# Expert passes of an fp32 MoE block: small-block groups one chunk sooner, one-hot picks on VectorE, two weight remainders on GpSimd

## The reference, cut to what matters

```python
logits = h @ w_router + b_router
top_v, top_i = lax.top_k(logits, 4); gates = softmax(top_v)
# tokens of each expert, in blocks of rows; for each block (idx, gate, e):
xb = xt[idx]
g = min(xb @ w_gate[e] + b_gate[e], 7.0)
u = clip(xb @ w_up[e] + b_up[e], -7.0, 7.0)
act = g * sigmoid(1.702 * g) * (u + 1)
y = (act @ w_down[e] + b_down[e]) * gate[:, None]
# the rows of y are added to their tokens
```

## Time and profile before

| | us |
|---|---|
| median of 3 runs | 2213.45 |
| lowest, highest | 2213.32, 2217.33 |
| the profiled execution | 2214.42 |
| its span, first to last instruction | 2212.7 |
| TensorE busy | 2137.0 (97%) |
| VectorE busy | 1538.9 (70%) |
| ScalarE busy | 1114.8 (50%) |
| GpSimd busy | 888.5 (40%) |
| mean granted TensorE clock | 0.988 |

### The profile page before, as it was taken

How to read it: one execution, slowest core, us unless ns; L and a number is a source line. 1 busy time by engine, 2 the same in 40 slices (tenths; PEclk the granted TensorE clock), 3 DMA queues, 4 the chain that set the end, 5 groups by cost and what they waited for, 6 DMA issues and landing times.

```text
span 2212.7 us, 37038 instructions
## 1 busy us (share of the span) xinstructions
PE 2137.0 (97%) x11540; PEld 1557.8 (70%) x11541; DVE 1538.9 (70%) x1940; ACT 1114.8 (50%) x1138; POOL 888.5 (40%) x486
## 2 busy tenths in 40 slices
PE   8999999999999969999999999999999999999997
PEld 6874554787888847777666767776776766677776
DVE  5544433535335588988777788878887877789996
ACT  4433233424222146675645656565665655566674
POOL 1343121000000045875633545555574455356761
PEclk9999999999999979999999999999999999999999
DMA  6421110233334289999878898899898898899994
GB/s 227 98 74 60 39 47 10 82 90 102 88 105 152 105 325 388 352 357 338 302 274 292 315 303 317 307 319 313 308 352 280 302 307 291 291 318 324 351 341 111
DMA packets 206010, 517.77 MB, mean 234 GB/s; under 512 B 19168, under 2 KB 86624, under 8 KB 205952
## 3 DMA queue, kind: packets, MB, share of 16 engines
q1 hardware_dynamic: 190016, 470.97, 59.2%
q0 software_dynamic: 15936, 46.02, 8.6%
HBM read 480.68 MB, written 32.05 MB: 232 GB/s over the span
## 4 chain that ended last, share of the span: by engine, by line
PE 69%; issue 8%; DVE 8%; POOL 8%; DMA 3%; DVEq 3%; ACT 1%; SPq 0%; POOLq 0%; ACTq 0%
PE psum L1689 7%; PE psum L1933 7%; PE psum L1924 6%; PE psum L1926 6%; PE psum L1901 5%; POOL pick L679 4%; PE psum L1709 4%; PE psum L1711 4%; PE psum L1710 4%; DVE late_lo L1385 3%; PE psum L1964 3%; PE psum L1966 3%; PE psum L1972 3%; PE psum L1912 2%; DMA out_rows<-ysb,idx_cur 2%
## 5 line engine op out<-in xcount | busy, mean ns | idle before, releaser
L679 POOL TENSOR_SCALAR pick<-iota_bf,slot_col 128x256 bf16<-128x256 bf16 x244 | 523.5, 2160 | 214.5 <-DVE slot_col L1403 214.5
L1385 DVE TENSOR_TENSOR late_lo<-late_raw,w_hi 128x2048 fp32r<-128x2048 f32 x192 | 433.2, 2291 | 121.9 <-PE psum L1972 83.2
L1385 DVE TENSOR_TENSOR ring_lo<-ring,w_hi 128x2048 fp32r<-128x2048 f32 x191 | 432.6, 2300 | 70.2 <-PE psum L1933 70.2
L922 ACT ACTIVATE w_hi<-late_raw 128x2048 fp32r<-128x2048 f32 x192 | 363.4, 1918 | 1.3 <-DMA late_raw<-in_w_up 0.8
L922 ACT ACTIVATE w_hi<-ring 128x2048 fp32r<-128x2048 f32 x192 | 354.2, 1922 | 9.9 <-DMA ring<-in_w_up 9.9
L1924 PE MATMUL psum<-w_hi,xT_hi 128*128 128x512 f32 x992 | 270.4, 394 | 0.8 <-DVE idx_new L1379 0.5
L1926 PE MATMUL psum<-w_hi,xT_lo 128*128 128x512 f32 x992 | 265.6, 389 | 0.0
L1924 PEld LDWEIGHTS psum<-w_hi,xT_hi 128*128 128x128 f32 x992 | 184.1, 188 | 46.5 <-issue 7.4
L1926 PEld LDWEIGHTS psum<-w_hi,xT_lo 128*128 128x128 f32 x992 | 186.2, 188 | 39.5
L1689 PE MATMUL psum<-hT,ring 128*128 128x512 f32 x384 | 174.2, 601 | 0.0
L653 POOL TENSOR_TENSOR rstd<-var,half 128x1 f32<-128x1 f32 x8 | 4.4, 554 | 409.5 <-DVE var L1327 409.5
(11 more groups left out here) (362 smaller groups left out, 3706.0 us busy)
## 6 DMA issues: line engine op xcount, KB each, us to landing
late_raw<-in_w_down SPq DMA_DIRECT2D x132, 512.0 KB, 4.6
ring<-in_w_gate SPq DMA_DIRECT2D x130, 512.0 KB, 4.3
ring<-in_w_up SPq DMA_DIRECT2D x130, 512.0 KB, 5.4
late_raw<-in_w_gate SPq DMA_DIRECT2D x126, 512.0 KB, 6.0
late_raw<-in_w_up SPq DMA_DIRECT2D x126, 512.0 KB, 7.7
ring<-in_w_down SPq DMA_DIRECT2D x124, 512.0 KB, 5.0
ring<-in_w_in SPq DMA_DIRECT2D x44, 512.0 KB, 5.1
ring<-in_x SPq DMA_DIRECT2D x16, 512.0 KB, 4.0
```

The lines of the kernel that those rows point to most:

```text
L679: e.tensor_scalar(pick[:, t, :], iota_bf[:, :], slot_col[:, t, :], None, ALU.is_equal).then_inc(g_pick, 1)
L922: e.activation(w_hi[:, hs, :], raw_of(c0), ACT.Copy).then_inc(g_hi, 1)
L1385: e.tensor_tensor(lo_of(c0), raw_of(c0), w_hi[:, hs, :].bitcast(F32), ALU.subtract).then_inc(g_lo, 1)
```

## The change

In the loop, `second_rows` stands in chunk k=1 and not 2, `down_rows` in k=5 and not 6, `next_rows` in c=2 and not 3, and `rows_transpose` behind c=0 and not c=1. The eight picks move from GpSimd to VectorE, right behind `slots_of`. The remainders of chunks 18 and 19 move from VectorE to GpSimd, which reads the flag `hb` for it and raises a semaphore of their own, `g_lo_pool`; since VectorE makes 10 remainders in a pass now and not 12, `g_lo` is counted anew. `row_numbers` stands behind the remainder of chunk 20. In `gate_up`, the two products that write bank 3 stand last, behind the wait for `g_rows`. The two changed places of the small groups are also in the gate-and-up product behind the loop. The core of the diff:

```diff
@@ gpsimd, loop
-                pick_tokens(p + 3)
+                hb = e.value_load(table[0:1, bass.ds(p + NT, 1)], min_val=0, max_val=1)
+                for c in range(2, 4):
+                    hold(e, g_hi, 12 * p + (17 + c))
+                    if c == 2:
+                        with e.If(hb > 0):
+                            hold(e, g_small, 3 * p + 5)
+                    e.tensor_tensor(lo_of(16 + c), raw_of(16 + c), w_hi[:, (16 + c) % SPLIT, :].bitcast(F32), ALU.subtract).then_inc(g_lo_pool, 1)
@@ vector, loop
                 slots_of(p + 3, exn)
+                e.wait_ge(g_col, p + 3)
+                for t in range(TT):
+                    e.tensor_scalar(pick[:, t, :], iota_bf[:, :], slot_col[:, t, :], None, ALU.is_equal).then_inc(g_pick, 1)
...
                 evacuate(p + 1, hbn, 12 * p + 16)
-                for c in range(2, 4):
-                    rest_of_weights(p, 16 + c)
                 rest_of_rows(p + 2, xT_hi, xT_lo, 0)
                 shift_rows(p, False)
-                row_numbers(p + 3, 3)
                 small_taken(hb2, 3 * p + 6)
                 rest_of_weights(p, 12 + 8)
+                row_numbers(p + 3, 3)
@@ tensor, gate_up
-                for i in range(4):
+                for i in range(3):
...
-                for i in range(4):
+                for i in range(3):
                     e.matmul(bank[i][:, :], lo[:, k, :], w_hi[:, hs, 512 * i:512 * i + 512], start=False, stop=False)
+                if numbers is not None:
+                    e.wait_ge(g_rows, numbers)
+                e.matmul(bank[3][:, :], hi[:, k, :], w_hi[:, hs, 1536:2048], start=(k == 0), stop=False)
+                e.matmul(bank[3][:, :], lo[:, k, :], w_hi[:, hs, 1536:2048], start=False, stop=False)
@@ tensor, down
-                e.wait_ge(g_lo, at + 1)
+                if of_pool is not None:
+                    e.wait_ge(g_lo_pool, of_pool)
+                else:
+                    e.wait_ge(g_lo, 10 * p + (c0 + 1))
@@ tensor, loop
-                    gate_up(p, 8 + k, k, aside={2: second_rows, 6: down_rows}.get(k), signals_small=k in (2, 6))
+                    gate_up(p, 8 + k, k, aside={1: second_rows, 5: down_rows}.get(k), signals_small=k in (1, 5))
...
-                    down(p, 16 + c, c, aside={1: third_expert, 3: next_rows}.get(c), signals_small=c == 3)
-                    if c == 1:
+                    down(p, 16 + c, c, aside={1: third_expert, 2: next_rows}.get(c), signals_small=c == 2, of_pool=2 * p + (c - 1) if c >= 2 else None)
+                    if c == 0:
                         rows_transpose(p + 2, 0, 2)
```

More of the change, by code:

```diff
@@ L343, in build @@
         first_lo = sem("first_lo")
-        g_warm = sem("g_warm"); g_hi = sem("g_hi"); g_lo = sem("g_lo"); g_chunk = sem("g_chunk"); g_small = sem("g_small")
+        g_warm = sem("g_warm"); g_hi = sem("g_hi"); g_lo = sem("g_lo"); g_chunk = sem("g_chunk"); g_small = sem("g_small"); g_lo_pool = sem("g_lo_pool")
         g_bgu = sem("g_bgu"); g_bd = sem("g_bd")
@@ L1918, in gate_up @@
                 e.wait_ge(g_hi, at + 1)
-                for i in range(4):
+                for i in range(3):
                     if halves and i == 2:
                         e.wait_ge(g_ev, 2 * p + 2)
-                    if numbers is not None and i == 3:
-                        e.wait_ge(g_rows, numbers)
                     e.matmul(bank[i][:, :], hi[:, k, :], w_hi[:, hs, 512 * i:512 * i + 512], start=(k == 0), stop=False)
-                for i in range(4):
+                for i in range(3):
                     e.matmul(bank[i][:, :], lo[:, k, :], w_hi[:, hs, 512 * i:512 * i + 512], start=False, stop=False)
+                if numbers is not None:
+                    e.wait_ge(g_rows, numbers)
+                e.matmul(bank[3][:, :], hi[:, k, :], w_hi[:, hs, 1536:2048], start=(k == 0), stop=False)
+                e.matmul(bank[3][:, :], lo[:, k, :], w_hi[:, hs, 1536:2048], start=False, stop=False)
                 if aside:
@@ L1957, in act_transpose, with down @@
                 ins.then_inc(g_atr, 1)
-            def down(p, c0, c, aside=None, signals_small=False):
+            def down(p, c0, c, aside=None, signals_small=False, of_pool=None):
                 at, slot, hs, _ = chunk_at(p, c0)
@@ L2068, in part @@
                     if h == 0:
-                        e.wait_ge(g_lo, at + 1)
+                        e.wait_ge(g_lo, 10 * n_loop + (21 + c))
                     for k in (2 * c, 2 * c + 1):
@@ L2101, in _ @@
             for k in range(1, GU_CHUNKS):
-                gate_up(n_loop, 8 + k, k, aside={2: last_second_rows, 6: last_down_rows}.get(k), signals_small=k in (2, 6))
+                gate_up(n_loop, 8 + k, k, aside={1: last_second_rows, 5: last_down_rows}.get(k), signals_small=k in (1, 5))
                 if k == 3:
```

2 lines of the change are left out of this document (1 added, 1 removed).

## The result

| | us |
|---|---|
| before, median of 4 runs | 2213.94 |
| changed kernel, median of 4 runs | 2280.23 (2279.75 to 2280.72) |
| ratio, 95% interval | 1.030 (1.0288 to 1.0313) |
| the profiled execution's span, before and after | 2212.7, 2278.6 |
| mean granted TensorE clock, before and after | 0.988, 0.978 |

The changed kernel is 66 us slower. The forecast was 97 us slower, 2310 us, with a range of 2270 to 2335. The direction and one mechanism were right, but the working was not: two terms were too large, one cost of 31 us had been put at nothing, and that the time still lies in the range is in part luck, since the errors partly cancelled.

What follows compares the result with a forecast made beforehand. VectorE was taken to set passes without groups, TensorE mostly the others. By kinds +51, +22, +17 and -6 made +84; the clock's +13 gave +97 on 2214.4, from the median 2310 us; own range 2270 to 2335, wider range 2225 to 2345.

Steps and rivals of the forecast that it cites:

- Sooner groups: TensorE's waits for late remainders go: 1.2 us less with all groups, 2.3 with gate-and-up, 1.9 with down_rows alone.
- VectorE's work, -2.6 us: Per pass, two remainders of 2.2 us leave VectorE and eight picks, 1.85 us with the slots' wait, come.
- The lock: GpSimd and VectorE exclude each other for whole instructions on SBUF; GpSimd's chunk 18 remainder holds VectorE 4.7 us, delaying evacuate.
- GpSimd waits for the very signal that lets VectorE begin remainder 16, so the collision is certain: In passes with down_rows the lock always strikes; with down_rows alone +2.5 us each, times 7 is +17.
- The lock holds these for 4.7 us: VectorE's remainders 15 to 17 and everything behind are held; passes without groups grow 6.4 us, times 8 is +51.
- the pick of the earlier trace: A GpSimd pick of 0.92 us took 4.82, asked for 0.4 us into VectorE's first remainder, letting the second pass.
- The first rival: The lock costs VectorE nothing, GpSimd getting in only at pauses or PSUM reads: 2189 us, faster; chance 0.14.
- Chunk 19's remainder, taken as hidden: GpSimd makes it in the 7.3 us behind evacuate, ending at about the next T (slot_rows), so it hides.
- From the end of `evacuate` the order is fixed ... 7.3 to the next T: Without groups: transposes 1.2, chunk 17 2.6, chunk 18 2.9, slot_rows 0.5 us to the next T, slot_rows.
- The later `row_numbers` ... These I take at nothing: row_numbers behind remainder 20 moves the gather 2.3 us back, its rows wanted some 30 us on: no cost.
- The sooner transpose: It needs evacuate's end; slack 0.65 us against a chunk of 2.7, so TensorE waits, 4 us in 23 passes with the lock.
- The clock: Behind the new waits TensorE's granted clock dips, 1.7 us each, 7 or 8 more dips: +13 us (-7 to +32).

Runs made afterwards that it cites:

- e3: The kernel before with only the sooner groups (second_rows at k=1, down_rows at k=5, next_rows at c=2): 2187.3 us.
- e11: The kernel before with sooner groups, picks on VectorE and bank 3 written last; transpose, two remainders and row_numbers as before: 2189.1 us.
- e6: The changed kernel with both remainders back on VectorE behind evacuate and rows_transpose back behind c == 1: 2220.2 us.
- e1: The changed kernel with the remainders of chunks 18 and 19 back on VectorE, right behind evacuate: 2231.3 us.
- e5: The kernel before with only the eight picks moved from GpSimd to VectorE, behind slots_of: 2210.8 us.
- e13: The changed kernel with the transpose back behind c == 1, row_numbers back ahead of remainder 20, and GpSimd's remainders in quarters: 2210.2 us.
- e8: The changed kernel with row_numbers back ahead of remainder 20: 2248.1 us.
- e12: The kernel before with only row_numbers moved behind remainder 20 and bank 3's two products last: 2305.8 us.
- e2: The changed kernel with rows_transpose back behind c == 1: 2252.0 us.
- e10: The changed kernel with each of GpSimd's two remainders made in four instructions of 128 x 512: 2257.2 us.
- e4: The changed kernel with GpSimd's remainder of chunk 18 waiting for the first half of evacuate: 2272.2 us.

## Why the prediction was right and wrong

By a ladder of kernels, each one edit from the next, the change is:

| step | us |
|---|---|
| before | 2212.9 |
| sooner groups (e3) | -25.6 |
| picks on VectorE, bank 3 last (e11) | +1.8 |
| `row_numbers` behind remainder 20 (e6) | +31.1 |
| transpose one chunk sooner (e1) | +11.1 |
| two remainders on GpSimd (changed) | +48.9 |
| sum | 2280.2 |

- **Sooner groups**: forecast -39, measured -26. The term was mis-sized for `down_rows` passes (1.9 against 0.5), since TensorE's time laid end to end is not what bounds them.
- **VectorE's work, -2.6 us**: the picks were worked out as 1.85 and took 1.66; on their own they cost nothing (e5). Right. But the two remainders that go freed little, since they had filled a wait for the transposed rows (e13).
- **The lock**: an exclusion for whole instructions, right, with 4.4 to 4.6 us each, right. "GpSimd waits for the very signal that lets VectorE begin remainder 16, so the collision is certain" held in 8 of 15 passes; in the other 7 VectorE was mid-run when GpSimd asked. "The lock holds these for 4.7 us" in passes without groups was the step that failed: the pick of the earlier trace rows had shown that GpSimd waits for more than the instruction in hand, and I used that only for the gate-and-up passes. The first rival's mechanism was true in 22 of 30 passes; its price was wrong, since it too left out the turn of the loop, the held casts and the 8 passes where GpSimd is first. For passes without groups it had 40.5 to 40.7 us, and with `row_numbers` back ahead of remainder 20 they measure 40.48 (e8).
- **Chunk 19's remainder, taken as hidden**: it wasn't quite. `shift_rows` did wait for it, as written, but that wait is on the way that sets a pass without groups: 1.2 us in each (e1).
- **"From the end of `evacuate` the order is fixed ... 7.3 to the next T"**: a true sum on TensorE, and not the way that sets a pass without groups. That one runs on VectorE: remainder 9 to the end of `evacuate` (918.34 to 946.62, 28.3 us), then `rest_of_rows`, `shift_rows`, remainder 20, `row_numbers` and the stop, to the next remainder 9 (960.66, 14.0 us), together 42.3. The forecast was 45.2 for a mean of 41.9.
- **"The later `row_numbers` ... These I take at nothing"**: the largest miss, 31 us. I followed the gathered rows (wanted 30 us on, true) and didn't ask what stands last in VectorE's loop. The 1.10 us of "issue" in front of the first instruction of the earlier trace rows were the sign: they are the part of a turn of 3.3 us that remainder 20 doesn't cover. GpSimd's issue of the gathers, which the expectations of e8, e11 and e12 take for the cause, only falls at the same time, since the end of `row_numbers` starts both.

The gathers are held up by VectorE, not VectorE by them. Two gathers of the kernel before without VectorE's remainders, and two beside them:

```profile
1399.25 1.04 POOL L685 DMA_INDIRECT xg<-h_rows,idx_new  x1 [8.94 <-DVE idx_new L1379]
1400.60 0.98 POOL L687 DMA_INDIRECT xgb<-h_rows,idx_new  x1 [0.30 <-issue]
...
1444.58 2.38 POOL L685 DMA_INDIRECT xg<-h_rows,idx_new  x1 [6.05 <-DVE idx_new L1379]
1447.27 3.03 POOL L687 DMA_INDIRECT xgb<-h_rows,idx_new  x1 [0.30 <-issue]
```

- **The sooner transpose**: waits for `ut` came in 23 passes, the number of the forecast, but by luck: forecast were the 8 without groups, the 8 with all and the 7 with `down_rows`; measured are 8 without, 7 with gate-and-up groups, and the 3 and 5 locked ones. They are 3.1 to 3.7 us in 16 of them and 1.6 to 1.7 in the others, not 4. On its own the sooner transpose costs 11 us, and 28 with the lock in place (e2), none of it in the passes without groups.
- **The clock**: more dips came (mean clock 0.978 from 0.988), but in passes without groups they lay beside TensorE's spare time; e2 has them too and no pass there changed. The +13 can't be told apart from the waits and was at most partly real.
- By kinds the forecast was +6.4, +2.7, +2.5 and -0.9 for none, all, `down_rows` and gate-and-up; measured were +3.0, +1.0, +4.2 and +0.8. The sum held better than its parts: in passes without groups the lock that I had counted was absent, and the loop's turn and the held cast that I hadn't counted stood in its place.

Still open is what decides whether GpSimd or VectorE is served next when both have asked. The runs show both orders (e10), and no run was made on that alone.

## What to carry to other kernels

Find the engine whose round sets each kind of pass before pricing an edit: 3 us of TensorE's waiting were worth nothing in passes that VectorE set, and 1 us of small instructions moved behind one large one cost 2.2 in each of those. Let a loop's body end in a long instruction, which covers the turn of the loop and the values that it loads. Before moving work off an engine, ask whether it stood in a wait: two remainders taken off VectorE (4.4 us a pass) and made by GpSimd in 9.2 cost 21 us even with the three costs mended. Price a helper that shares a port by what it holds up, down to casts of two columns.

## What the runs showed of the hardware

- A remainder of 128 x 2048 is 4.60 to 4.64 us on GpSimd when nothing is in its way, 2.29 on VectorE. Asked for in the middle of a run of VectorE's remainders it took up to 10.6 us.
- A cast of two columns on VectorE (L1439, one SBUF input, 0.16 us alone) was held by GpSimd's remainders too and took 1.7 to 2.4 us in the changed kernel and up to 4.0 in e4; copies of two and four columns took up to 1.35 in e13. `evacuate`, which reads PSUM, was never held: each of its two large instructions took 1.21 to 1.23 us in the changed kernel. The Trainium skill (SBUF — State Buffer, Who interferes with whom) lists copy and cast among the instructions that can take the shared pair, and the trace agrees.
- Issuing an indirect DMA on GpSimd is held up by VectorE's two-operand remainders, and not the other way round. In the kernel before, the first gather took 2.33 to 2.41 us the 15 times that a remainder was in hand, and 1.01 to 1.11 the 17 times that none was. The 97 remainders that run beside an indirect issue in the changed kernel all took 2.29 us or less. The same section infers that a `tensor_tensor` and descriptor generation don't meet, since one takes only reads and the other needs writes. The trace shows the longer issue beside a `tensor_tensor` in every kernel here; but an indirect issue also reads its row numbers (`idx_new`) from SBUF, and no run tells which of the two is held.
- The turn of VectorE's loop, with four values loaded from `table` at some 0.3 us each and their checks, took 3.30 us of its sequencer (median of 30 turns, the same within 0.01 us in all 13 kernels). It shows as idle time of "issue", 1.1 us behind a remainder of 2.29 and 3.3 behind an instruction of 0.15.
- A run of quarter-size instructions on GpSimd lets VectorE in between: two remainders of VectorE took 6.68 us beside it, against 8.90 beside one whole instruction and 4.49 alone.
